# Rounding the feed-forward's gated tile in its own block instead of the next one

## The chip, the cores and the metric

The kernel runs on one core of a Trainium2 chip. The metric is device time in microseconds for one execution. All arithmetic is in 32-bit floats; matrix products are done as three products of split operands.

## What is computed

Two blocks of a network on 256 tokens of width 1024: a first block of two layers (a recurrent mixer in layer 0, a windowed attention in layer 1, each followed by a gated feed-forward part), and a second block with two kinds of attention on 16 further meta tokens. The change concerns the feed-forward part of both layers:

```python
D_MODEL = 1024
SEQ = 256
D_FF = -(-(8 * D_MODEL) // (3 * 256)) * 256      # 2816 = 11 blocks of 256

def swiglu(h, w_in, w_out):
    gu = h @ w_in
    gate, up = gu[..., :D_FF], gu[..., D_FF:]
    return (jax.nn.silu(gate) * up) @ w_out

x = x + swiglu(rmsnorm(x, norm_ffn_w[i]), ffn_w_in[i], ffn_w_out[i])
```

## The kernel before

The five engines have hand-written programs that meet in semaphores. Each engine works through its own list in order, so a wait also holds what stands behind it.

**Split operands.** Every operand of a product is a pair: a rounded part (hi) and what is left (the rest, lo). `mm3` (L472) issues three matmuls, hi by hi, hi by lo and lo by hi. ACT makes the hi part by a copy into the rounded type, DVE makes the lo part by a subtraction.

**Main weights** come in 56 chunks of 1024 x 512, each as two halves of 1 MB. SP loads a half into `w_raw` (one buffer for each half, `main`, L347) once DVE has made the rest of the same half of the chunk before; ACT rounds it into `w_hi` (`split_main`, L1210), DVE makes `w_lo` (`rest_main`, L1742). `w_hi` and `w_lo` have two slots. **Side units** are 128 x 1024 pieces, for the feed-forward's down projection two for each block; they have two slots too (`s_raw`, `s_hi`, `s_lo`), and SP loads the next one into a slot when DVE has made the rest of the one there (`side`, L352). SP's order is: both halves of a main chunk, then two side units, then the next chunk.

**The feed-forward part** has 11 blocks of 256 hidden features (`ffn` on each engine: L728 on TensorE, L1417 on ACT, L2089 on DVE). The order on TensorE (PE) is written out by hand: up(f+1), then down(f).

- `up(f)` (L740): 96 matmuls of 256 columns give gate and up rows of the block, for each of two halves of 128 features in one PSUM bank.
- ACT and DVE gate: DVE scales a half out of its bank into `ffn_nat` (L2097), ACT takes the silu in place (`gate`, L1423), DVE multiplies (L2103).
- The gated tile is `ffn_nat[:, 1]`. ACT rounds it into g_hi (`rounded`, L1430), DVE makes g_lo (`rested`, L2116). There is one such pair of tiles, so `rounded(f)` waits on `s_used` until down(f-1), which reads it, is over.
- `down(f)` (L751): waits for g_lo, then for each of the two side units waits for its s_lo and issues 12 matmuls of 512 columns into four banks that sum over all blocks. Each unit's last matmul signals `s_used`.

Block f on ACT and DVE (`block_`, L1432 and L2118) stands as: round and rest the gated tile of block **f-1**; gate block f; split the main chunk of block f+2; split the two side units of block f. The last block (f = 10) has a place of its own for its gated tile (`last_gh`, `last_gl`, in x_hi and x_lo) and its second side unit (`last_sh`, `last_sl`), and rounds the tile between the two side units:

```python
for s in range(2):
    slot = (u0 + s) % 2
    hi = s_hi[:, slot, :]
    if last and s:
        rounded(f, last_gh)
        hi = last_sh
    else:
        act.wait_ge(s_used, u0 + 2 * f + s - 2)
```

Behind the last block ACT and DVE split the next chunk (L1275, L1838), DVE adds the four banks into the residual h (L2152), and TensorE transposes h for what follows (L545), in the middle of `last_down` (L763).

Block 0 is written out before the loop, in the order gate, side units, round and rest, chunk 2.

Of the kernel before, what the change touches and what calls it, by code (L numbers as in the profile page):

```python
# [163 lines left out]
def two_blocks(nc, w_main, w_side, params, rows, c_l0, c_l1, c_b2, ident_d, x_d, x_t, meta_d, pos_d, out_d):  # L164
    ctx = ExitStack()
    with ctx:
# [40 lines left out]
        def side_raw(slot, quarters=False):  # L207
            return s_raw[:, slot, :].rearrange("p (k t) -> p k t", k=4) if quarters else s_raw[:, slot, :]
# [62 lines left out]
        last_gh, last_gl, last_sh, last_sl = x_hi[:, 2:4, M:L], x_lo[:, 2:4, M:L], x_hi[:, 4:8, M:L], x_lo[:, 4:8, M:L]  # L271
# [937 lines left out]
        def _(act):  # L1209
            def split_main(c, slot):  # L1210

                for g in range(2):
                    act.wait_ge(w_landed[g], 16 * c + 16)
                    act.activation(w_hi[:, slot, 4 * g:4 * g + 4, :], w_raw[:, g, :, :], ACT.Copy).then_inc(w_hi_ok, 1)  # L1214

            def split_side(u, after=None):

                act.wait_ge(s_landed[u % 2], 16 * (u // 2 + 1))
                if after is not None:
                    act.wait_ge(acc_ready[USE[after] % 2], USE[after] // 2 + 1)  # L1220
                act.activation(s_hi[:, u % 2, :], s_raw[:, u % 2, :], ACT.Copy).then_inc(s_hi_ok, 1)
# [51 lines left out]
            def split_half(c, slot, g):  # L1273
                act.wait_ge(w_landed[g], 16 * c + 16)
                act.activation(w_hi[:, slot, 4 * g:4 * g + 4, :], w_raw[:, g, :, :], ACT.Copy).then_inc(w_hi_ok, 1)  # L1275
# [134 lines left out]
            def meta_pairs():  # L1410

                for t, k0, k1 in ((meta_hi, 0, META_G), (meta_lo, META_G, KT)):
                    act.activation(t[:, :, 0:M], x_hi[:, k0:k1, 0:M], ACT.Copy)
                    act.activation(t[:, :, 2 * M:3 * M], x_lo[:, k0:k1, 0:M], ACT.Copy)
                act.drain().then_inc(xm_ok, 1)

            def ffn(layer, after):  # L1417
                c0, u0, n0 = C_FFN[layer], U_DOWN[layer], USE[(f"ffn{layer}", 0, 0)]

                def gate(f):  # L1420
                    for half in range(2):
                        act.wait_ge(acc_free[(n0 + half) % 2], (n0 + half) // 2 + f + 1)
                        act.activation(ffn_nat[:, 0, half, :], ffn_nat[:, 0, half, :], ACT.Silu).then_inc(silu_ok, 1)  # L1423

                def rounded(f, hi=ffh, first=False):

                    act.wait_ge(gated_ok, 2 * FB * layer + 2 * f + 2)
                    if not first:
                        act.wait_ge(s_used, u0 + 2 * f - 1)
                    act.activation(hi, ffn_nat[:, 1, :, :], ACT.Copy).then_inc(g_hi_ok, 1)  # L1430

                def block_(f, j, last=False, first=False):  # L1432
                    if not first:
                        rounded(f - 1)
                    gate(f)
                    if not last:
                        split_main(c0 + f + 2, (c0 + j) % 2)
                    for s in range(2):
                        slot = (u0 + s) % 2
                        hi = s_hi[:, slot, :]  # L1440
                        if last and s:
                            rounded(f, last_gh)
                            hi = last_sh
                        else:
                            act.wait_ge(s_used, u0 + 2 * f + s - 2)
                        act.wait_ge(s_landed[slot], 16 * (f + (u0 + s) // 2 + 1))
                        act.activation(hi, side_raw(slot, last and s), ACT.Copy).then_inc(s_hi_ok, 1)

                act.wait_ge(rb_ps, 1 + 2 * layer)
                act.activation(root_row, bank[6][:, 0:S], ACT.Copy).then_inc(root_ok, 1)  # L1450
                gate(0)
                for s in range(2):
                    split_side(u0 + s)
                rounded(0, first=True)
                split_main(c0 + 2, c0 % 2)
                block_(1, 1, first=True)
                if layer == 0:

                    act.wait_ge(meta_landed, 16)
                    act.activation(um[0:M, :], hm[0:M, :], ACT.Square, accum_out=stat[0:M, 0:1]).then_inc(ss_ok, 1)  # L1460
                else:
                    act.wait_ge(um_lo, 1)
                    meta_pairs()
                block_(2, 2)
                with act.Fori(1, (FB - 1) // 2 - 1) as i:
                    block_(2 * i + 1, 1)
                    block_(2 * i + 2, 2)
                if layer == 0:

                    act.wait_ge(ang_ok, 1)  # L1470
                    act.activation(sinT, ang[:, 0, :], ACT.Sin)
                    act.activation(cosT, ang[:, 1, :], ACT.Sin).then_inc(tab_ok, 1)

                block_(FB - 2, 1)
                block_(FB - 1, 2, last=True)
                for g in range(2):
                    split_half(c0 + FB + 1, c0 % 2, g)
                after()
# [13 lines left out]


            ffn(0, x1)

            acc_in(("ak",))
# [46 lines left out]
            def u_():  # L1543
# [18 lines left out]
                next_sides(1, (1,))  # L1562

            ffn(1, u_)


# [174 lines left out]
        def _(dve):  # L1741
# [162 lines left out]
            last = [P - 1, P]  # L1904
# [184 lines left out]
            def ffn(layer, first_tiles, after):  # L2089
# [24 lines left out]
                def rested(f, hi=ffh, lo=ffl):  # L2114
                    dve.wait_ge(g_hi_ok, FB * layer + f + 1)
                    dve.tensor_tensor(lo, ffn_nat[:, 1, :, :], hi, ALU.subtract).then_inc(g_lo_ok, 1)  # L2116

                def block_(f, j, last=False, first=False, between=None):  # L2118
                    if not first:
                        rested(f - 1)  # L2120
                    gated_halves(f, between)
                    if not last:
                        rest_main(c0 + f + 2, (c0 + j) % 2)
                    for s in range(2):
                        slot = (u0 + s) % 2
                        hi, lo = s_hi[:, slot, :], s_lo[:, slot, :]
                        if last and s:
                            rested(f, last_gh, last_gl)
                            hi, lo = last_sh, last_sl
                        dve.wait_ge(s_hi_ok, u0 + 2 * f + s + 1)  # L2130
                        dve.tensor_tensor(lo, side_raw(slot, last and s), hi, ALU.subtract).then_inc(s_lo_ok, 1)  # L2131
# [4 lines left out]
                    rest_side(u0 + s)  # L2136
                rested(0)
                rest_main(c0 + 2, c0 % 2)
                block_(1, 1, first=True)
                block_(2, 2, between=angles if layer == 0 else None)  # L2140
                with dve.Fori(1, (FB - 1) // 2 - 1) as i:
                    block_(2 * i + 1, 1)
# [573 lines left out]
```

## Time and profile before

| | |
|---|---|
| time, median of 3 runs | 954.61 us (954.53 to 956.06) |
| time of the profiled execution | 956.59 us |
| its span, from the first to the last instruction | 954.8 us |
| TensorE's matmuls (PE) busy | 97% of the span |
| DVE busy | 63% |
| ACT busy | 50% |
| bytes moved by DMA | 150.51 MB, 158 GB/s on average |

Times in the profile are microseconds from the start of the span. A timeline row has the start, the duration, the engine, the line of the kernel, the operation and, in brackets, how long the engine had been idle before it and what ended that. A matmul's own duration is modelled and overlaps the next one's; starts are the better reading. An idle engine costs nothing unless something that bounds the end waits for it. Layer 0's feed-forward stage runs from about 130 to 325 us, layer 1's from about 420 to 610.

### The profile page before, as it was taken

The numbers are of one execution on the slowest core, as the hardware profiler recorded it, in microseconds if no ns is written. First come the engines' busy times: TensorE is split into PE (matmuls) and PEld (weight loads), VectorE is DVE, ScalarE is ACT, GpSimd is POOL, SyncE is SP. The second block draws the span as 40 slices with busy tenths as digits, with TensorE's granted clock in tenths as the row PEclk, the third lists the DMA queues.
The fourth block names the chain that finished last, engine by engine and source line by source line (L and its number), as shares of the span: only waits on it lengthen the run. The fifth ranks groups of instructions, "written<-read, shape, count | busy, mean of one in ns | idle before, by whom it ended". The sixth has DMA issues, their size and how long they took to land.

```text
span 954.8 us, 15686 instructions
## 1 busy us (share of the span) xinstructions
PE 927.1 (97%) x6013; PEld 818.6 (86%) x6013; DVE 606.0 (63%) x1099; ACT 479.5 (50%) x781; POOL 38.8 (4%) x67
## 2 busy tenths in 40 slices
PE   6999899999999999999999999999999999999997
PEld 6887689999998798899999999789987878878776
DVE  5866857746557678557546556676665556565665
ACT  6555565334344547555334343677354454445443
POOL 1013200000000000000000000001011000000000
PEclk9999999999999999999999999999999999999999
DMA  8552346553644622236553644531523242533441
GB/s 310 207 184 81 108 176 220 181 217 132 233 162 155 243 89 90 89 131 220 180 217 132 223 173 164 189 132 71 199 90 134 89 162 104 176 119 126 176 176 44
DMA packets 26380, 150.51 MB, mean 158 GB/s; under 512 B 3664, under 2 KB 3920, under 8 KB 12112
## 3 DMA queue, kind: packets, MB, share of 16 engines
q1 hardware_dynamic: 24912, 147.44, 42.6%
q0 software_dynamic: 1408, 2.25, 0.8%
q8 instruction: 40, 0.66, 0.3%
q14 instruction: 20, 0.16, 0.1%
HBM read 148.50 MB, written 1.05 MB: 157 GB/s over the span
## 4 chain that ended last, share of the span: by engine, by line
PE 46%; DMA 18%; DVE 17%; ACT 10%; issue 4%; SPq 2%; DVEq 2%; ACTq 0%
DMA w_raw<-w_main_dram 18%; PE bank L474 12%; PE bank L476 11%; PE bank L475 11%; ACT w_hi L1214 5%; DVE s_lo L2131 4%; DVE w_lo L1746 4%; DVE w_lo L1838 2%; PE bank L545 1%; PE bank L1028 1%; DVE arena L2238 1%; SPq L345 1%; ACT w_hi L1275 1%; PE bank L1043 1%; PE bank L1081 1%
## 5 line engine op out<-in xcount | busy, mean ns | idle before, releaser
L474 PE MATMUL bank<-x_hi,w_hi 128*128 128x256 f32 (+1 forms) x976 | 279.2, 286 | 9.3 <-DVE w_lo L1848 8.0
L475 PE MATMUL bank<-x_lo,w_hi 128*128 128x256 f32 (+1 forms) x976 | 274.1, 281 | 0.0
L476 PE MATMUL bank<-x_hi,w_lo 128*128 128x256 f32 (+1 forms) x976 | 273.7, 280 | 0.0
L474 PEld LDWEIGHTS bank<-x_hi,w_hi 128*128 128x128 f32 x976 | 184.6, 189 | 13.0 <-issue 9.3
L1746 DVE TENSOR_TENSOR w_lo<-w_raw,w_hi 128x2048 fp32r<-128x2048 f32 x50 | 114.3, 2291 | 113.4 <-ACT w_hi L1214 112.8
L475 PEld LDWEIGHTS bank<-x_lo,w_hi 128*128 128x128 f32 x976 | 184.8, 189 | 0.8
L476 PEld LDWEIGHTS bank<-x_hi,w_lo 128*128 128x128 f32 x976 | 184.7, 189 | 0.0
L1214 ACT ACTIVATE w_hi<-w_raw 128x2048 fp32r<-128x2048 f32 x54 | 103.1, 1916 | 112.0 <-DMA w_raw<-w_main_dram 106.0
L474 PE MATMUL bank<-w_hi,x_hi 128*128 128x512 f32 (+2 forms) x296 | 119.1, 402 | 0.8 <-DVE w_lo L1746 0.8
L1838 DVE TENSOR_TENSOR w_lo<-w_raw,w_hi 128x2048 fp32r<-128x2048 f32 x51 | 116.2, 2283 | 5.5 <-ACT w_hi L1275 5.4
L475 PE MATMUL bank<-w_lo,x_hi 128*128 128x512 f32 (+2 forms) x296 | 112.6, 380 | 0.0
L476 PE MATMUL bank<-w_hi,x_lo 128*128 128x512 f32 (+2 forms) x296 | 112.5, 380 | 0.0
L1275 ACT ACTIVATE w_hi<-w_raw 128x2048 fp32r<-128x2048 f32 x50 | 95.1, 1907 | 17.2 <-DMA w_raw<-w_main_dram 16.7
L1423 ACT ACTIVATE ffn_nat<-ffn_nat 128x256 f32<-128x256 f32 x44 | 18.4, 418 | 108.3 <-DVE ffn_nat L2097 108.3
L474 PE MATMUL bank<-s_hi,g_hi 128*128 128x512 f32 x166 | 66.3, 399 | 2.4 <-DVE g_lo L2116 1.8
L474 PEld LDWEIGHTS bank<-w_hi,x_hi 128*128 128x128 f32 x296 | 55.8, 188 | 13.6 <-issue 4.1
L1504 ACT ACTIVATE arena<-arena,small 128x144 f32<-128x144 f32 x64 | 29.5, 461 | 74.4 <-DVE small L2215 74.3
L476 PE MATMUL bank<-s_hi,g_lo 128*128 128x512 f32 x166 | 65.5, 395 | 0.0
L476 PEld LDWEIGHTS bank<-w_hi,x_lo 128*128 128x128 f32 x296 | 55.6, 188 | 11.5
L475 PE MATMUL bank<-s_lo,g_hi 128*128 128x512 f32 x166 | 65.3, 393 | 0.0
L475 PEld LDWEIGHTS bank<-w_lo,x_hi 128*128 128x128 f32 x296 | 55.8, 189 | 8.6
L474 PE MATMUL bank<-w_hi,s_hi 128*128 128x512 f32 x128 | 53.2, 415 | 0.7 <-DVE h L2029 0.4
(378 smaller groups left out, 1436.5 us busy)
## 6 DMA issues: line engine op xcount, KB each, us to landing
w_raw<-w_main_dram SPq DMA_DIRECT2D x111, 1024.0 KB, 5.2
s_raw<-w_side_dram SPq DMA_DIRECT2D x51, 512.0 KB, 4.2
w_raw<-w_main_dram SPq DMA_DIRECT2D x2, 512.0 KB, 6.1
h<-x_dram SPq DMA_DIRECT2D x2, 512.0 KB, 10.5
arena<-rows_dram POOLq DMA_DIRECT2D x2, 512.0 KB, 4.3
arena<-x_t_dram SPq DMA_DIRECT2D x1, 768.0 KB, 6.7
out_dram<-arena SPq DMA_DIRECT2D x1, 512.0 KB, 2.6
out_dram<-arena SPq DMA_DIRECT2D x2, 256.0 KB, 2.1
```

The lines of the kernel that those rows point to most:

```text
L345: sp.dma_start(dst, w_main[c, g]).then_inc(w_landed[g], 16)
L474: pe.matmul(out, ah, bh, start=first, stop=False)
L475: pe.matmul(out, ah, bl, start=False, stop=False)
L476: return pe.matmul(out, al, bh, start=False, stop=last)
L545: ins = pe.transpose(b[:, M + r * P:M + (r + 1) * P], src(r, k), ident[:, :])
L1214: act.activation(w_hi[:, slot, 4 * g:4 * g + 4, :], w_raw[:, g, :, :], ACT.Copy).then_inc(w_hi_ok, 1)
L1275: act.activation(w_hi[:, slot, 4 * g:4 * g + 4, :], w_raw[:, g, :, :], ACT.Copy).then_inc(w_hi_ok, 1)
L1423: act.activation(ffn_nat[:, 0, half, :], ffn_nat[:, 0, half, :], ACT.Silu).then_inc(silu_ok, 1)
L1504: ins = act.activation(tiles(r), tiles(r), ACT.Exp, bias=small[:, s0 + 2 + r:s0 + 3 + r], accum_out=small[:, s0 + 4 + r:s0 + 5 + r])
L1746: dve.tensor_tensor(w_lo[:, slot, 4 * g:4 * g + 4, :], w_raw[:, g, :, :], w_hi[:, slot, 4 * g:4 * g + 4, :], ALU.subtract).then_inc(w_lo_o ...
L1838: dve.tensor_tensor(w_lo[:, slot, 4 * g:4 * g + 4, :], w_raw[:, g, :, :], w_hi[:, slot, 4 * g:4 * g + 4, :], ALU.subtract).then_inc(w_lo_o ...
L2131: dve.tensor_tensor(lo, side_raw(slot, last and s), hi, ALU.subtract).then_inc(s_lo_ok, 1)
```

## The change

The gated tile of block f is rounded and rested inside block f, right behind its gating, ahead of the main chunk and the side units, on ACT and on DVE. The last block does the same with its own tile, so there the rounding stands ahead of both side units. Block 0 stays as it was. What each instruction waits for is the same as before.

```diff
-                def block_(f, j, last=False, first=False):
-                    if not first:
-                        rounded(f - 1)
+                def block_(f, j, last=False):
                     gate(f)
-                    if not last:
+                    if last:
+                        rounded(f, last_gh)
+                    else:
+                        rounded(f)
                         split_main(c0 + f + 2, (c0 + j) % 2)
                     for s in range(2):
                         slot = (u0 + s) % 2
                         hi = s_hi[:, slot, :]
                         if last and s:
-                            rounded(f, last_gh)
                             hi = last_sh
                         else:
                             act.wait_ge(s_used, u0 + 2 * f + s - 2)
...
-                block_(1, 1, first=True)
+                block_(1, 1)
...
-                def block_(f, j, last=False, first=False, between=None):
-                    if not first:
-                        rested(f - 1)
+                def block_(f, j, last=False, between=None):
                     gated_halves(f, between)
-                    if not last:
+                    if last:
+                        rested(f, last_gh, last_gl)
+                    else:
+                        rested(f)
                         rest_main(c0 + f + 2, (c0 + j) % 2)
                     for s in range(2):
                         slot = (u0 + s) % 2
                         hi, lo = s_hi[:, slot, :], s_lo[:, slot, :]
                         if last and s:
-                            rested(f, last_gh, last_gl)
                             hi, lo = last_sh, last_sl
```

ACT's list at the first block of layer 0 and the head of its loop, before (w_hi: main chunk, s_hi: side unit, ffn_nat: silu, g_hi: rounding of the gated tile):

```order
 L1430 ACTIVATE g_hi<-ffn_nat 128x512
 L1214 ACTIVATE w_hi<-w_raw 128x2048 x2
 L1423 ACTIVATE ffn_nat<-ffn_nat 128x256 x2
 L1214 ACTIVATE w_hi<-w_raw 128x2048 x2
 L1447 ACTIVATE s_hi<-s_raw 128x1024 x2
```

and with the change:

```order
 L1430 ACTIVATE g_hi<-ffn_nat 128x512
 L1214 ACTIVATE w_hi<-w_raw 128x2048 x2
 L1423 ACTIVATE ffn_nat<-ffn_nat 128x256 x2
 L1430 ACTIVATE g_hi<-ffn_nat 128x512
 L1214 ACTIVATE w_hi<-w_raw 128x2048 x2
 L1447 ACTIVATE s_hi<-s_raw 128x1024 x2
```

The rounding of block 1 now stands between its silus and the split of the chunk; before, it followed the side units, as the first item of block 2.

ACT's list at the end of layer 0's feed-forward part, from the rounding of block 9 on, before (x_hi<-ffn_nat: rounding of the last gated tile, x_hi<-s_raw: the last side unit, w_hi at L1275: the next chunk):

```order
 L1430 ACTIVATE g_hi<-ffn_nat 128x512
 L1423 ACTIVATE ffn_nat<-ffn_nat 128x256 x2
 L1447 ACTIVATE s_hi<-s_raw 128x1024
 L1430 ACTIVATE x_hi<-ffn_nat 128x2x256
 L1447 ACTIVATE x_hi<-s_raw 128x4x256
 L1275 ACTIVATE w_hi<-w_raw 128x2048 x2
```

and with the change:

```order
 L1423 ACTIVATE ffn_nat<-ffn_nat 128x256 x2
 L1430 ACTIVATE x_hi<-ffn_nat 128x2x256
 L1447 ACTIVATE s_hi<-s_raw 128x1024
 L1447 ACTIVATE x_hi<-s_raw 128x4x256
 L1275 ACTIVATE w_hi<-w_raw 128x2048 x2
```

The rounding of block 9 has moved up into its own block, and the last rounding from between the two side units to ahead of both. DVE's rests (L2116, L1746, L2131) move in the same way in every block.

## Rows read from the trace of the kernel before

**Rows 1.** The page: busy time of the engines, and the chain that ended last.
```profile
PE 927.1 (97%) x6013; PEld 818.6 (86%) x6013; DVE 606.0 (63%) x1099; ACT 479.5 (50%) x781; POOL 38.8 (4%) x67
...
PE 46%; DMA 18%; DVE 17%; ACT 10%; issue 4%; SPq 2%; DVEq 2%; ACTq 0%
```

**Rows 2.** Timeline, TensorE: down(2)'s last matmul, down(3)'s first and last, layer 0.
```profile
195.20 0.39 PE L476 MATMUL bank<-s_hi,g_lo 128*128 128x512 f32 x1
...
206.66 0.39 PE L474 MATMUL bank<-s_hi,g_hi 128*128 128x512 f32 x1
...
211.98 0.39 PE L476 MATMUL bank<-s_hi,g_lo 128*128 128x512 f32 x1
```

**Rows 3.** Chain in order of time: start, duration, what; two flights are second halves.
```profile
215.19 1.93 ACT w_hi L1214
...
223.29 8.87 DMA w_raw<-w_main_dram
...
456.82 10.24 DMA w_raw<-w_main_dram
```

**Rows 4.** Timeline, ACT and DVE, the same block: first half, side rests, g_lo.
```profile
212.74 1.92 ACT L1214 ACTIVATE w_hi<-w_raw 128x2048 fp32r<-128x2048 f32 x1 [4.74 <-DMA w_raw<-w_main_dram]
...
219.35 2.35 DVE L2131 TENSOR_TENSOR s_lo<-s_raw,s_hi 128x1024 fp32r<-128x1024 f32 x2
221.62 0.68 DVE L2116 TENSOR_TENSOR g_lo<-ffn_nat,g_hi 128x512 fp32r<-128x512 f32 x1
```

**Rows 5.** TensorE's waits over the whole run: us in total, times, longest.
```profile
PE bank L474 <- DVE x_lo L2116: 3.0, 2, 1.5
PE bank L474 <- DVE g_lo L2116: 1.8, 4, 1.1
```

**Rows 6.** Timeline, TensorE: last matmul of down(0) and down(9), both layers.
```profile
161.64 0.39 PE L476 MATMUL bank<-s_hi,g_lo 128*128 128x512 f32 x1
...
314.57 0.40 PE L476 MATMUL bank<-s_hi,g_lo 128*128 128x512 f32 x1
...
446.70 0.39 PE L476 MATMUL bank<-s_hi,g_lo 128*128 128x512 f32 x1
...
599.87 0.40 PE L476 MATMUL bank<-s_hi,g_lo 128*128 128x512 f32 x1
```

**Rows 7.** Timeline, DVE: rest of the chunk's second half in block 1, both layers.
```profile
165.30 2.29 DVE L1746 TENSOR_TENSOR w_lo<-w_raw,w_hi 128x2048 fp32r<-128x2048 f32 x1 [0.73 <-ACT w_hi L1214]
...
450.65 2.29 DVE L1746 TENSOR_TENSOR w_lo<-w_raw,w_hi 128x2048 fp32r<-128x2048 f32 x1 [0.28 <-ACT w_hi L1214]
```

**Rows 8.** Timeline, ACT, DVE and TensorE: the last block of layer 0.
```profile
312.22 1.06 ACT L1447 ACTIVATE s_hi<-s_raw 128x1024 fp32r<-128x1024 f32 x1 [0.45 <-PE bank L476]
315.06 0.63 ACT L1430 ACTIVATE x_hi<-ffn_nat 128x512 fp32r<-128x512 f32 x1 [1.78 <-PE bank L476]
315.60 1.04 ACT L1447 ACTIVATE x_hi<-s_raw 128x1024 fp32r<-128x1024 f32 x1
316.54 1.90 ACT L1275 ACTIVATE w_hi<-w_raw 128x2048 fp32r<-128x2048 f32 x1
...
313.31 1.23 DVE L2131 TENSOR_TENSOR s_lo<-s_raw,s_hi 128x1024 fp32r<-128x1024 f32 x1 [1.08 <-ACT s_hi L1447]
...
320.69 1.28 DVE L2152 TENSOR_TENSOR h<-h,bank 128x512 f32<-128x512 f32 x2
...
316.47 0.50 PE L474 MATMUL bank<-s_hi,x_hi 128*128 128x512 f32 x1 [1.50 <-DVE x_lo L2116]
...
321.29 0.40 PE L476 MATMUL bank<-x_hi,x_lo 128*128 128x512 f32 x1
322.02 0.66 PE L545 MATMUL bank<-ident,h 128*128 128x128 f32 x4 [0.34 <-DVE h L2152]
```

**Rows 9.** Windows: length, busy us of the engines, PEclk, DMA share, GB/s.
```profile
8.00:14.00 6.00, 6.00 (x29) 6.00 (x30) 4.21 (x9) 3.98 (x9) 0.00 (x0) 1.00 1.02 418
...
314.00:318.00 4.00, 2.50 (x12) 1.54 (x10) 2.46 (x3) 2.94 (x3) 0.00 (x0) 1.00 0.99 408
```

More of the change, by code:

```diff
@@ L2138, in ffn @@
                 rest_main(c0 + 2, c0 % 2)
-                block_(1, 1, first=True)
+                block_(1, 1)
                 block_(2, 2, between=angles if layer == 0 else None)
```

## The prediction

> **What bounds the kernel now.** I read the page first, then the matmuls in order of time, then ACT, DVE and the waits of the feed-forward stages. TensorE is busy for 97% of the span, yet the chain that ended last gives 18% of the span to the loads of the main weights and 17% to DVE [rows 1]. Two things run at nearly one speed, then. Nothing outside the two feed-forward stages is touched, so the question is where TensorE stops inside them.
>
> *TensorE's pace.* The last matmul of one down projection starts at 195.20, that of the next at 211.98 [rows 2]: a block takes **16.78 us** when nothing is waited for.
>
> *The weight loop's pace.* A chunk's second half lands, ACT splits it (1.93 from 215.19 on), DVE takes the rest (from 1.95 after ACT's start), then the rests of both side units, and only behind these does SP issue the next loads: the next second half is on its way from 223.29 for 8.87 and lands at 232.16, when ACT can start again, 0.03 later [rows 3]. That is a round of **17.00 us**. The loop falls behind TensorE by 0.22 us a block, and by more where a flight takes longer (10.24 in layer 1 [rows 3]).
>
> *What ends the waits.* The rest of the gated tile, g_lo, is DVE's last item in that loop: it ends at 222.30, and TensorE wants it at 223.44 [rows 4]. As the loop falls behind, this margin goes. TensorE waits for g_lo four times, up to 1.1 us [rows 5]. The whole loss is read better from first and last matmul: layer 0 from 161.64 to 314.57 is 152.93 us for nine blocks, where nine times 16.78 is 151.02, so 1.91 us lost; layer 1 from 446.70 to 599.87 is 153.17, so 2.15 us [rows 6]. Behind that each layer has one wait of 1.5 us for x_lo, the last gated tile [rows 5].
>
> **The change part by part.** No arithmetic is added or taken away: in each layer the roundings and rests of blocks 1 to 9 (18 of each in all) and of the last block (2 of each) move. PE, SP and POOL keep their order. A rounding takes ACT 0.63 us [rows 8], a rest takes DVE 0.68 [rows 4].
>
> *The gain: g_lo comes before the wait that mattered.* Let the lead be ACT's start on a second half minus the start of the last matmul of the down projection before it: 215.19 - 211.98 = 3.21. TensorE reaches the next down projection 11.46 after that matmul (195.20 to 206.66 [rows 2]). Before, it needs g_lo, which ends 222.30 - 215.19 = 7.11 after ACT's start and is seen 0.05 later, so it stalls once the lead passes 11.46 - 7.16 = 4.30. Afterwards g_lo is long there, and what ends last is the rest of the **first side unit**. It ends 219.35 + 1.23 - 215.19 = 5.39 after ACT's start [rows 4, 8], so the stall begins at a lead of 11.46 - 5.44 = 6.02. (The second unit is wanted 12 matmuls, some 2.8 us, later and is 1.2 us behind the first: never last.) That is 1.72 us more room in each layer.
>
> *The price inside the loop: the first block.* `rounded(f)` waits for the down projection of f-1 to be over, since it overwrites the tile that this reads. ACT sees that end 0.49 us after the last matmul's start (314.57 to 315.06 [rows 8]). Behind it ACT now holds the split of the next chunk. With the rounding on ACT for 0.54 before the next start (315.06 to 315.60), that split cannot start earlier than 1.03 after the last matmul. In steady blocks this costs nothing: 211.98 + 1.03 = 213.01 against 212.74, and the second half is not ready before 215.19 anyway [rows 4]. DVE then takes the second half's rest at the old time, to 0.01 us. But in block 1 the loads came early, as the loop had just started. In layer 0 the first half was split as soon as it had landed, now at 161.64 + 1.03 = 162.67; DVE starts that rest 1.95 later, at 164.62, and the second at 166.83 (a rest takes 2.29, and the next item starts 0.08 before its end, as 221.62 against 221.70 [rows 4]), where it was 165.30: **1.53 us**. In layer 1: 446.70 + 1.03 = 447.73, rests at 449.68 and 451.89 instead of 450.65: **1.24 us** [rows 6, 7]. The loop feeds itself (the side rests are late, so SP issues late), so the delay stays in it for the other eight blocks.
>
> So the stalls are 1.91 + 1.53 - 1.72 = 1.72 us in layer 0 and 2.15 + 1.24 - 1.72 = 1.67 in layer 1. **Gains: 0.19 and 0.48.** Bounds: nothing if the flights grow a little, 1.72 per layer if the loop catches up after block 1. I take the middle of the mechanism, since [rows 3] show no slack in the loop.
>
> *The price in the last block.* Before, ACT splits the block's first side unit (s_hi) during the down projection, at 312.22, and the rounding into x_hi follows at 315.06. TensorE restarts at 316.47, 1.90 after its last matmul (314.57), on x_lo. Now the rounding stands first and still waits for the down projection's end. Counted from 314.57: rounding 0.49 to 1.12, s_hi 1.03 to 2.09; on DVE x_lo 1.15 to 1.84 and s_lo 2.12 to 3.35 [rows 8]. TensorE restarts at 3.40 instead of 1.90: **1.50 us later**, waiting for s_lo. Some of it is covered: at 322.02 (7.45) TensorE waited for DVE's sum into h, though its own work would have let it go on at 321.29 + 0.23, 6.95 (0.23 is the step of the 512-column matmuls, 5.32 us for 23 of them [rows 2]). Now its own work brings it there at 8.45. The sum is queued behind the split of the next chunk, which ACT starts 0.94 later (one more unit ahead of it) and DVE too, so it ends at 7.40 + 0.94 = 8.34. TensorE goes on at 8.45 instead of 7.45: **1.0 us late**. I take 1.0 per layer, with bounds 0.9 and 1.5 and nothing to take off, since behind it TensorE is full [rows 1].
>
> *SP's queue.* The next layer's side loads are issued behind those rests, and come some 2 us later; the main load behind them waits for the chunk's rest and moves by 0.94 with it. That is inside the 1.0 already.
>
> *Sum:* -0.19 - 0.48 + 1.0 + 1.0 = **+1.3 us**. The profiled execution took 956.59 us around a span of 954.8; by the sum it would be 957.9 and the span 956.1. The runs' median is 954.61, 2 us under the profiled one, so the forecast is **955.9 us**. That is 0.14% and would not be told from no change: 0.2%, about 1.9 us, is what a measurement of this kernel can tell.
>
> **A rule of the skill against the row.** The gaps of TensorE end on g_lo, and the edit makes just that value earlier [rows 5]. The Trainium skill, Perfetto Trace Analysis, section Optimization Strategy, says to look at the gaps of the limiting engine, find the signal that ends them and let what sends it start sooner; read so, the stalls of 4.06 us would be the gain. The trace disagrees in part: the loop of [rows 3], not g_lo, falls behind.
>
> **The rivals.**
> - *B, the loop catches up.* The delay of block 1 is not carried, because flights after it are shorter. Against it: the loop's round of 17.00 has no idle step in it. For it: in layer 1 the flight after block 1 took 10.24 [rows 3], so something disturbs it that a shift might miss. Then 1.72 is recovered twice: -3.44 + 2.0 = -1.4 us, 953.2. With the last block covered as well, -3.4 us, 951.2.
> - *S, the last block is paid in full (slower).* Place: the restart on s_lo behind block 10. If the sum into h ends half a microsecond later than worked out, the cover is gone and 1.50 counts twice: 3.0 - 0.7 = +2.3 us, 956.9; with no stall recovered +3.0, 957.6. It decides from 1.3 us a layer on. For it: the sum stands only 0.1 us ahead of TensorE, behind five queued items on DVE. Against it: their times repeat to 0.01 us in both layers.
> - *C, the clock.* TensorE's gap there grows from 1.9 to 3.4 us from start to start. The granted clock reads 1.00 (the 2.4 GHz level) in the stretch with the present gap. It does in the first stretch too, though there 29 matmuls take 6.00 us, 0.21 each [rows 9], where 96 of them take 11.46 - 0.23, 0.12 each [rows 2]. If the longer gap brought that slow stretch back, 29 x (0.21 - 0.12) = 2.6 us more per layer: 1.3 + 5.2 = +6.5 us, 961.1. The Trainium skill, TensorE: Matmul & The Clock Gate, section Why this matters for your kernels, warns that idle gaps between bursts return the engine to its slow level. No row here shows it in a running stage.
> - *N, nothing changes in effect,* because TensorE still meets the second limit each time: 954.6.
>
> **How the numbers follow.** Forecast 0.52, S 0.22, B 0.13 and its far form 0.05, C 0.04, N 0.04. Of the forecast's own spread 0.04 lies over 0.2% slower; of B 0.02 over 0.2% faster. So slower 0.22 + 0.04 + 0.04 = 0.30, faster 0.05 + 0.02 = 0.07, the same 0.63. The range holds B to S with the run-to-run spread: 952.9 to 957.8.
>
> **What would show it.** In the new trace: ACT's split of the first half in block 1 starts about 1.0 us behind the last matmul of the down projection, and the lead in block 2 is 1.2 to 1.5 us larger than it was; leads reach 6 and more by block 8; TensorE's waits before down projections name s_lo, not g_lo, and still sum to about 1.7 us a layer; the last down projection starts 3.4 us after the one before ended, on s_lo; h comes 1 us later. I am wrong if the leads fall back after block 2 (B), if TensorE goes on 1.5 us late after the last block (S), or if matmuls behind it start further apart than 0.23 us (C).

## The result, and the profile after

| | before | after |
|---|---|---|
| median of the runs, us | 955.02 (951.15 to 956.06, 6 runs) | 960.18 (958.46 to 963.0, 6 runs) |
| ratio to before | | 1.006 (95%: 1.0037 to 1.0083) |
| profiled execution: time, span, us | 956.59, 954.8 | 958.46, 956.7 |
| mean granted clock, mean of the runs | 0.9991 | 0.9943 |
| stages (last matmul of down(0) to that of down(9)), us | 152.93, 153.17 | 151.02, 151.48 |
| TensorE's restart behind down(9), us after its start | 1.90, 1.90 | 3.47, 3.48 |
| first transpose of h, counted likewise, us | 7.45, 7.45 | 9.98, 9.29 |

The change makes the kernel slower by 0.6%, 5.2 us; 955.9 with a range up to 957.8 was forecast. The profiled execution of the changed kernel is the fastest of its six, so the traces show only 1.9 us of it. Clock means here and below are over all executions of a kernel in its comparison; the one for before is over the 30 that ran beside experiments 1 to 4.

The page: TensorE as busy as before, but the chain that ended last now runs over TensorE for 63% and over the loads for 11%, where it was 46% and 18% [rows 1]. In the middle of the stages nothing but TensorE sets the pace.
```profile
PE 927.2 (97%) x6013; PEld 819.7 (86%) x6013; DVE 605.7 (63%) x1099; ACT 480.3 (50%) x781; POOL 38.8 (4%) x67
...
PE 63%; DVE 12%; DMA 11%; ACT 7%; issue 3%; DVEq 2%; SPq 1%; ACTq 0%
```

Timeline, TensorE: the last matmuls of down(0) and down(9) in both layers, as in [rows 6].
```profile
162.45 0.39 PE L476 MATMUL bank<-s_hi,g_lo 128*128 128x512 f32 x1
...
313.47 0.39 PE L476 MATMUL bank<-s_hi,g_lo 128*128 128x512 f32 x1
...
448.07 0.39 PE L476 MATMUL bank<-s_hi,g_lo 128*128 128x512 f32 x1
...
599.55 0.40 PE L476 MATMUL bank<-s_hi,g_lo 128*128 128x512 f32 x1
```
Layer 0 takes 151.02 us, which is nine times 16.78 with no stall at all; layer 1 takes 151.48. Against [rows 6] the stages gain 1.91 and 1.69 us. And yet from down(9) of layer 0 to down(0) of layer 1 it is 134.60 us instead of 132.13, so 2.47 lost, and from down(9) of layer 1 to the end of the span 357.15 instead of 354.93, 2.22 lost. A further 0.81 is lost ahead of down(0), in a stretch that the edit doesn't touch (over the twelve traces of this case down(0) ends anywhere from 160.31 to 162.51). -1.91 + 2.47 - 1.69 + 2.22 + 0.81 = +1.9, the difference of the spans. So, apart from that 0.81, all that is lost is lost behind the two last blocks.

TensorE's waits: us in total, times, longest. The rows of x_lo and of L2116's g_lo [rows 5] are gone, and one for s_lo has come.
```profile
PE bank L474 <- DVE s_lo L2131: 6.2, 2, 3.1
...
PE bank L545 <- DVE h L2152: 0.7, 1, 0.7
```

Timeline, ACT and DVE, block 1 of layer 0, then ACT's split of the second half in block 9.
```profile
162.94 0.63 ACT L1430 ACTIVATE g_hi<-ffn_nat 128x512 fp32r<-128x512 f32 x1 [2.30 <-PE bank L476]
163.47 3.71 ACT L1214 ACTIVATE w_hi<-w_raw 128x2048 fp32r<-128x2048 f32 x2
163.60 0.69 DVE L2116 TENSOR_TENSOR g_lo<-ffn_nat,g_hi 128x512 fp32r<-128x512 f32 x1 [2.51 <-ACT g_hi L1430]
165.41 4.49 DVE L1746 TENSOR_TENSOR w_lo<-w_raw,w_hi 128x2048 fp32r<-128x2048 f32 x2 [1.11 <-ACT w_hi L1214]
...
300.82 1.92 ACT L1214 ACTIVATE w_hi<-w_raw 128x2048 fp32r<-128x2048 f32 x1 [0.54 <-DMA w_raw<-w_main_dram]
```
The rounding holds the split until 163.47, which is 1.02 after the matmul of 162.45 (1.03 was worked out). The two rests start 2.96 and, 2.2 later, some 5.17 behind it; the second was at 3.66 [rows 6, 7], so the push is 1.51 us, as forecast (1.53). It isn't carried in this trace, though. The lead (ACT's second split behind the last matmul of the down projection before) is 3.14 in block 2 and 300.82 - 296.69 = 4.13 in block 9, where before it rose from 2.01 to 5.57. In layer 1 it goes from 3.73 to 6.01 in block 8 and 6.18 in block 9, and behind these two stand the stalls that are left, 0.16 and 0.30 us. So TensorE stalls from a lead of about 5.87 on, where 6.02 was worked out; in the kernel before a lead of 5.57 went with a stall of 1.38, a limit of 4.19 where 4.30 was worked out. The room between the two limits is 1.68, as forecast (1.72).

Timeline, the last block of layer 0, ACT and DVE, then TensorE. Its counterpart is [rows 8].
```profile
313.95 0.63 ACT L1430 ACTIVATE x_hi<-ffn_nat 128x512 fp32r<-128x512 f32 x1 [4.05 <-PE bank L476]
314.49 1.04 ACT L1447 ACTIVATE s_hi<-s_raw 128x1024 fp32r<-128x1024 f32 x1
314.62 0.69 DVE L2116 TENSOR_TENSOR x_lo<-ffn_nat,x_hi 128x512 fp32r<-128x512 f32 x1 [4.26 <-ACT x_hi L1430]
315.44 1.04 ACT L1447 ACTIVATE x_hi<-s_raw 128x1024 fp32r<-128x1024 f32 x1
315.56 1.23 DVE L2131 TENSOR_TENSOR s_lo<-s_raw,s_hi 128x1024 fp32r<-128x1024 f32 x1 [0.26 <-ACT s_hi L1447]
...
316.94 0.47 PE L474 MATMUL bank<-s_hi,x_hi 128*128 128x512 f32 x1 [3.08 <-DVE s_lo L2131]
317.71 0.39 PE L474 MATMUL bank<-s_hi,x_hi 128*128 128x512 f32 x1
317.94 0.59 PE L475 MATMUL bank<-s_lo,x_hi 128*128 128x512 f32 x1
318.32 0.63 PE L476 MATMUL bank<-s_hi,x_lo 128*128 128x512 f32 x1
318.75 0.63 PE L474 MATMUL bank<-x_hi 128*128 128x512 f32 x1
...
321.31 0.43 PE L474 MATMUL bank<-s_hi,x_hi 128*128 128x512 f32 x1
321.58 0.40 PE L475 MATMUL bank<-s_lo,x_hi 128*128 128x512 f32 x1
```
Item by item this is what was worked out: the rounding waits for the down projection, s_hi and s_lo queue up behind it, and TensorE restarts 316.94 - 313.47 = 3.47 later (3.40). What was not in the sum comes next. The first matmuls follow each other at 0.23, and from 317.94 on at 0.43, eight of them, until 321.31; then at 0.23 again. That stretch costs 321.31 - 317.94 - 8 x 0.23 = 1.5 us. Below, matmuls that start that far apart are called slow.

Windows of the changed kernel: length, busy us of the engines, granted clock (the third number from the end), DMA share, GB/s.
```profile
314.00:318.00 4.00, 1.06 (x5) 0.92 (x6) 3.05 (x3) 4.00 (x4) 0.00 (x0) 1.00 0.57 215
318.00:322.00 4.00, 4.00 (x12) 3.13 (x11) 2.74 (x2) 2.08 (x2) 0.00 (x0) 0.58 0.84 268
```
The granted clock in the window behind the gap is 0.58: mostly the lower of its two levels (0.50, 1.2 GHz), for the rest the full one (1.00, 2.4 GHz). In the same four microseconds TensorE is called fully busy, which is why its busy share on the page tells nothing.

Timeline, the same place in layer 1, where the clock stayed up.
```profile
603.35 1.92 ACT L1275 ACTIVATE w_hi<-w_raw 128x2048 fp32r<-128x2048 f32 x1 [0.78 <-DMA w_raw<-w_main_dram]
605.30 2.29 DVE L1838 TENSOR_TENSOR w_lo<-w_raw,w_hi 128x2048 fp32r<-128x2048 f32 x1 [1.28 <-ACT w_hi L1275]
607.51 1.28 DVE L2152 TENSOR_TENSOR h<-h,bank 128x512 f32<-128x512 f32 x2
608.84 0.33 PE L545 MATMUL bank<-ident,h 128*128 128x128 f32 x1 [0.73 <-DVE h L2152]
```
Here ACT waits 0.78 for the next main chunk to land, DVE's rest of it is late by that, and the sum into h is queued behind that rest. h is transposed at 9.29 instead of the 8.45 worked out.

So three things were to be told apart: the longer path of the last block, the clock, and the landing of the next chunk.

### The profile page after: what moved, and what is told of

It is laid out like the page before. It is cut to its first block, busy times and chain, and to the rows that moved or that the text cites. A ratio compares the mean times of both kernels' runs of the same rounds, so it can differ in the third digit from the quotient of the medians.

```text
span 956.7 us, 15686 instructions
## 1 busy us (share of the span) xinstructions
PE 927.2 (97%) x6013; PEld 819.7 (86%) x6013; DVE 605.7 (63%) x1099; ACT 480.3 (50%) x781; POOL 38.8 (4%) x67
## 4 chain that ended last, share of the span: by engine, by line
PE 63%; DVE 12%; DMA 11%; ACT 7%; issue 3%; DVEq 2%; SPq 1%; ACTq 0%
PE bank L474 18%; PE bank L475 17%; PE bank L476 17%; DMA w_raw<-w_main_dram 11%; ACT w_hi L1214 3%; DVE w_lo L1838 2%; DVE s_lo L2131 2%; DVE w_lo L1746 2%; PE bank L545 1%; PE bank L1028 1%; DVE arena L2238 1%; PE bank L1043 1%; PE bank L1081 1%; PE bank L885 1%; PE bank L1063 1%
## 5 line engine op out<-in xcount | busy, mean ns | idle before, releaser
L1746 DVE TENSOR_TENSOR w_lo<-w_raw,w_hi 128x2048 fp32r<-128x2048 f32 x50 | 114.0, 2291 | 49.9 <-ACT w_hi L1214 49.4
L1275 ACT ACTIVATE w_hi<-w_raw 128x2048 fp32r<-128x2048 f32 x50 | 95.0, 1907 | 19.1 <-DMA w_raw<-w_main_dram 18.6
```

Of the source, the lines that this page charges most:

```text
L1746: dve.tensor_tensor(w_lo[:, slot, 4 * g:4 * g + 4, :], w_raw[:, g, :, :], w_hi[:, slot, 4 * g:4 * g + 4, :], ALU.subtract).then_inc(w_lo_o ...
```

## The experiments

Four kernels ran beside 30 executions of the kernel before (955.25 median, 952.46 to 958.44), then four beside 27 (956.01, 952.27 to 959.61), then two beside 17 (955.36, 953.12 to 959.44). What a version costs against before is counted from the median beside which it ran. All diffs are against the kernel before unless said otherwise. In some kernels line numbers differ by up to five. "Restart" is TensorE's first matmul of the last down projection and "h" the first transpose of h, both counted from the last matmul of down(9) as in the table above.

**1. Only the inner half of the edit (blocks 1 to 9).** The last block keeps its old order.
```diff
-                def block_(f, j, last=False, first=False):
-                    if not first:
-                        rounded(f - 1)
+                def block_(f, j, last=False):
                     gate(f)
                     if not last:
+                        rounded(f)
                         split_main(c0 + f + 2, (c0 + j) % 2)
```
with `rested` moved in the same way on DVE.

> Blocks 1 to 9 as changed, the last block in its old order. Theory (path and clock): the inner blocks save the stalls (1.9 us in layer 0, 1.7 in layer 1 in the profiled execution of the change), the last block keeps its gap of 1.9 us, and no clock is lost: about 955.0 - 3.6 = 951.4 us, granted clock as before. Rival (the inner order itself is slower in most executions, through longer flights of the weights): 957 us or more.

Measured: 956.67 us, ratio 1.0022 (1.0007 to 1.0037). My theory missed: this half alone makes the kernel slower by 1.4 us. The stages do take 151.50 and 151.67, so 1.43 and 1.50 us of stall are gone, and TensorE restarts at 1.90 as before. But h is transposed at 9.08 and 8.57 instead of 7.45, which gives back 1.63 and 1.12 of the 2.93 (one trace of each kernel). Timeline of this kernel, behind the last block of layer 0 (its last matmul of the down projection starts at 312.33), and a window behind that:
```profile
315.92 1.92 ACT L1275 ACTIVATE w_hi<-w_raw 128x2048 fp32r<-128x2048 f32 x1 [1.52 <-DMA w_raw<-w_main_dram]
317.87 2.29 DVE L1837 TENSOR_TENSOR w_lo<-w_raw,w_hi 128x2048 fp32r<-128x2048 f32 x1 [2.21 <-ACT w_hi L1275]
...
321.41 0.66 PE L545 MATMUL bank<-ident,h 128*128 128x128 f32 x4 [1.97 <-DVE h L2150]
```
```profile
322.00:327.00 5.00, 4.75 (x25) 4.29 (x24) 2.55 (x5) 1.65 (x4) 0.00 (x0) 0.66 0.43 180
```
TensorE arrives earlier, the load doesn't. The wait that was in front of the down projections stands behind the last block instead. And after the two gaps there (1.51 on x_lo, 1.97 on h) the granted clock fell too, to 0.66 over five microseconds, which cost 1.5 us more in this execution. Over its 12 executions the mean clock is 0.9978 against 0.9991; by an estimate that takes the lost clock as lost time, (0.9991 - 0.9978) x 955 = 1.2 us, about what the kernel is slower by.

The same trace shows a lead unlike that of the changed kernel, with the same inner order. ACT's split of the second half in blocks 2 and 9 of layer 0:
```profile
181.43 1.92 ACT L1214 ACTIVATE w_hi<-w_raw 128x2048 fp32r<-128x2048 f32 x1 [0.49 <-DMA w_raw<-w_main_dram]
...
301.41 1.92 ACT L1214 ACTIVATE w_hi<-w_raw 128x2048 fp32r<-128x2048 f32 x1 [0.54 <-DMA w_raw<-w_main_dram]
```
The down projections before them end at 177.61 and 295.26, so the lead goes from 3.82 to 6.15, where the changed kernel had 3.14 and 4.13.

**2. Only the last block's half of the edit.** On ACT, and likewise with `rested` on DVE:
```diff
-                    if not last:
+                    if last:
+                        rounded(f, last_gh)
+                    else:
                         split_main(c0 + f + 2, (c0 + j) % 2)
...
                         if last and s:
-                            rounded(f, last_gh)
                             hi = last_sh
```

> Only the last block as changed, blocks 1 to 9 in the old order. Theory (path and clock): TensorE's gap before the last down projection is 3.4 us in both layers, 1.6 us longer each, and the granted clock falls behind it in some executions; if the parts add up, 5.2 + 3.6 = 8.8 us over the kernel before, about 963.8 us, of which some 3.3 is the path and the rest clock. Path without clock: 958.3 us. Rival (the inner order is what costs): 955 to 956.5 us.

Measured: 960.28 us, ratio 1.0047 (1.0029 to 1.0064), the greater part of the whole change's 1.006. Alone this half costs 5.0 us; the sum of parts that I expected (963.8) is 3.5 too high, and the path without clock (958.3) is 2.0 too low. Restart at 3.47 in both layers, h at 9.76 and 11.23. Two lines of TensorE in layer 0, then a window in layer 1:
```profile
318.51 0.76 PE L474 MATMUL bank<-s_hi,x_hi 128*128 128x512 f32 x1 [3.08 <-DVE s_lo L2133]
319.07 0.63 PE L475 MATMUL bank<-s_lo,x_hi 128*128 128x512 f32 x1
```
```profile
606.00:608.00 2.00, 2.00 (x6) 1.58 (x5) 1.61 (x2) 2.00 (x2) 0.00 (x0) 0.50 0.85 266
```
In layer 1 the granted clock reads 0.50 in whole stretches, the lower level exactly. The slow matmuls cost 1.4 us in layer 0 and 2.8 in layer 1.

**3. The change, with the last rounding not waiting.** The wait protects the tile that the down projection before still reads. In the last block the rounding writes into another one (`last_gh`, a part of x_hi), so it needs no such wait. Against the changed kernel:
```diff
                     if last:
-                        rounded(f, last_gh)
+                        rounded(f, last_gh, first=True)
```

> The change, but the last block's rounding no longer waits for the down projection before it (its tile of its own does not need that wait), so it runs right behind the gating. Theory: TensorE's gap before the last down projection goes from 3.4 us to under 0.5, part of it moves to the wait for the sum into h; 1.2 us a layer less than with the old last block: about 949 us, granted clock as before. Rival (the inner order costs): 955 us or more.

Measured: 957.61 us, ratio 1.0023 (1.0009 to 1.0037), 8.6 above the expectation and in the rival's range. The gap did close, with restarts at 0.43 and 1.63. But TensorE then waits for the sum into h, 1.76 us in layer 0 and 3.27 in layer 1, and the sum is queued behind the late load. Timeline, layer 1:
```profile
607.08 0.65 PE L545 MATMUL bank<-ident,h 128*128 128x128 f32 x4 [3.27 <-DVE h L2152]
```
A gap of 3.27 on h has taken the place of the one that was removed, and slow matmuls follow it (608.04 to 611.47, 1.3 us).

**4. The change, with the gap filled.** Against the changed kernel, 12 matmuls of 512 columns ahead of the last down projection, into a bank that is free there. Their result isn't used.
```diff
                 def last_down(f):
+                    spare = w_hi[:, (c0 + FB) % 2, 0, :]
+                    pe.wait_ge(w_lo_ok, 2 * (c0 + FB) + 1)
+                    for _ in range(12):
+                        pe.matmul(bank[2][:, :], spare[:, 0:P], spare, start=True, stop=True)
                     pe.wait_ge(g_lo_ok, FB * layer + f + 1)
```

> The change, with 12 matmuls of 512 columns into an idle bank ahead of the wait of the last down projection (their result is not used), 2.8 us of work in a gap of 3.4 us. Clock theory: the path is as in the change, but the engine does not stand idle: about 954.7 to 956 us, granted clock 0.998 or more in every execution. Rival (the clock is no part of it, the 5.2 us are path): 960 us, as the change.

Measured: 956.44 us, ratio 1.0013 (1.0001 to 1.0026), where the change alone has 1.006. That is 1.2 us over before where the change has 5.2: 4.0 us are won by work of no use, which changes no wait and no order on ACT and DVE (3.7 between the two medians as they stand). The granted clock is 0.998 or more in all executions but the profiled one, which is the slowest of the 12 (0.997). Timeline and window behind the filled gap in layer 0; the last down projection itself restarts at 3.47, as in the change:
```profile
315.65 0.47 PE L474 MATMUL bank<-s_hi,x_hi 128*128 128x512 f32 x1 [0.34 <-DVE s_lo L2135]
```
```profile
318.00:322.00 4.00, 3.94 (x19) 2.76 (x18) 2.96 (x5) 1.67 (x3) 0.00 (x0) 1.00 0.76 227
```
h is transposed at 8.40, against 8.45 worked out. In layer 1 a late load still opens gaps further on (h at 10.59), and 1.4 us of slow matmuls follow there.

**5. Where the delay comes from: the order of the loads.** No edit of ACT or DVE. SP issues the next main chunk ahead of the two side units, and not behind them.
```diff
+                main(c0)
                 with sp.Fori(0, FB - 1) as i:
-                    main(c0 + i)
+                    main(c0 + i + 1)
                     for s in range(2):
                         side(u0 + 2 * i + s, (u0 + s) % 2)
```
(behind the loops, the main chunk that they have already issued is left out).

> The kernel before, with SP issuing the next main chunk ahead of the two side units in the feed-forward loops (nothing else). Theory W (the round main load, split, rests, side rests, next load is what falls behind TensorE, and it only hands its delay from place to place): the next chunk is issued about 4.7 us earlier in each round, so the stalls before the down projections go in the old order too, 1.9 + 2.1 us, and the last block keeps its gap of 1.9 us: about 951 us. Rival G (the late g_lo itself is the cause, as the change assumes): 955 us, stalls as before.

Measured: 952.43 us (951.83 to 953.23), ratio 0.9967 (0.9954 to 0.9981), faster than the kernel before, 1.4 above theory W and 2.6 below rival G. Both stages take 151.02 us, with g_lo still in its old place. TensorE's waits, then ACT and SP in the timeline:
```profile
PE bank L475 <- DVE x_lo L2117: 3.0, 2, 1.5
```
```profile
207.56 3.71 ACT L1215 ACTIVATE w_hi<-w_raw 128x2048 fp32r<-128x2048 f32 x2
...
224.34 3.71 ACT L1215 ACTIVATE w_hi<-w_raw 128x2048 fp32r<-128x2048 f32 x2
```
```profile
211.96 2.53 SPq L345 DMA_DIRECT2D w_raw<-w_main_dram  x2
215.30 1.47 SPq L354 DMA_DIRECT2D s_raw<-w_side_dram  x2
```
In the kernel before, the same block:
```profile
220.75 1.47 SPq L354 DMA_DIRECT2D s_raw<-w_side_dram  x2
222.77 0.85 SPq L345 DMA_DIRECT2D w_raw<-w_main_dram  x2
```
There SP stood at the side units until DVE had made their rests (219.35 and on [rows 4]) and came to the main chunk only then. Now ACT waits for no load; it waited 4.74 for the first half before [rows 4]. The round is 224.34 - 207.56 = 16.78, TensorE's own, where the loop had 17.00 [rows 3]. A kernel whose weight loop has room shows no stall on g_lo.

**6. The change on that load order.** Diffs of the change and of 5 together.

> The change with the same new order on SP. Theory W: no stall in the blocks, gap of 3.4 us before the last down projection, h 8.4 us behind it, clock lost as in the change: 951 + 2 (path of the last block) + 4 (clock) = about 957 us, and in the profile leads that no longer grow over the blocks. Rival G: 960 us, as the change.

Measured: 957.24 us, ratio 1.001 (0.9997 to 1.0023), so the change costs 4.8 us on this kernel also. Stages 151.02, restarts 3.47, h at 9.97 and 11.09, slow matmuls behind both gaps (1.5 and 2.7 us), as theory W had it. With no stall left to recover, only the last block's loss remains, and it is nearly as large as the change's 5.2 on the old order.

**7. That, with the last rounding not waiting.** Diffs of 6 and 3 together.

> As the run before, and the last block's rounding without the wait for the down projection. Theory W: no stall in the blocks, restart within 0.5 us, h about 7 us behind the end of the down projection: 951 - 2 x 0.5 = about 950 us if the clock holds, 952 if it falls in some executions. Rival G: 957 us, as the change with that wait gone.

Measured: 948.88 us (947.37 to 949.57), ratio 0.9921 (0.9902 to 0.9941). Restarts at 0.29 and 0.58, h at 5.43 and 5.70, no slow matmuls behind; 1.1 us under the 950 that was expected.

**8. Only the last block's half, with its gap filled.** Diffs of 2 and 4 together; the fillers' result isn't used.

> Only the last block as changed (blocks 1 to 9 old), with 12 matmuls of 512 columns filling TensorE's gap. Clock theory: the 3.4 us gap is bridged, the path cost of about 1 us a layer stays: 957 us, granted clock as in the kernel before. If the cost of the last block is all path: 960 us, as without the filling.

Measured: 957.0 us, ratio 1.0011 (0.9996 to 1.0025), where 2 had 1.0047, as the clock theory had it. The last down projection itself restarts at 3.48 in both layers, h at 8.42 and 8.45. The window in layer 1 that read 0.50 in 2:
```profile
606.00:608.00 2.00, 2.00 (x10) 1.65 (x9) 2.00 (x2) 1.78 (x1) 0.00 (x0) 1.00 0.89 272
```
TensorE is busy all of the two microseconds in both; it starts 10 instructions here and 6 there.

**9. The new load order with the inner half of the edit.** Diffs of 5 and 1 together.

> The kernel before with SP issuing the main chunk ahead of the side units, and the half of the change that lies in blocks 1 to 9 (the last block in the old order). Theory (the weight loop is what let TensorE fall behind, and with the loads in the new order the loop keeps up whatever the place of g_lo): both stages 151.0 us, no wait for g_lo, restart 1.90 behind the last down projection, time as the same load order without the edit, 952.4, within 1 us. Rival (the early g_lo is worth something by itself): 951 or less. Other rival (the split held behind the end of the down projection costs also here): 954 or more.

Measured: 952.41 us (951.56 to 953.5), ratio 0.9973 (0.9961 to 0.9985); stages 151.01 and 151.02, h at 7.45. The same as 5 within the intervals: an early g_lo is worth nothing once the loop keeps up, and costs nothing.

**10. The new load order, old inner order, last block rounded early without the wait.** Version 7 less its inner half.

> The new load order, the old order in blocks 1 to 9, and the last block as changed but with its rounding not waiting for the down projection before it. Theory (all that the best version gains over the load order comes from the last block): 948.9 within 1 us, stages 151.0, restart 0.3 to 0.6, no slow matmuls behind it. Rival (the inner half carries part of it): 950.5 or more.

Measured: 947.51 us (946.77 to 948.38), ratio 0.9923 (0.9903 to 0.9944), 1.4 under the expected 948.9, so a little outside its 1 us; it can't be told from 7. The page's chain, and TensorE at the end of layer 0's stage:
```profile
PE 82%; DVE 8%; ACT 5%; DMA 2%; DVEq 2%; issue 1%; ACTq 0%; SPq 0%
```
```profile
311.81 0.39 PE L477 MATMUL bank<-s_hi,g_lo 128*128 128x512 f32 x1
312.04 0.39 PE L475 MATMUL bank<-s_hi,x_hi 128*128 128x512 f32 x1
```
The last down projection follows the one before it at 0.23, with no gap, and h comes at 5.09 in both layers, 2.36 us earlier than in the kernel before. Twice that is 4.7, and from 9 to 10, which ran in one comparison, it is 4.9.

The three kernels with the open gap of 3.47 us (the change, 2 and 6), each with the one that differs from it in the filling or the wait alone, then 1 and the kernel before. In 4 and 8 the last down projection still restarts at 3.47 to 3.48, and the fillers start at 0.23. The kernel before had a mean clock of 0.9987 and 0.9988 in the later two comparisons.

| kernel | next matmul behind down(9), us | ratio to before | mean clock of its runs |
|---|---|---|---|
| the change | 3.47, 3.48 | 1.006 | 0.9943 |
| 4, the change, gap filled | 0.23, 0.23 | 1.0013 | 0.9988 |
| 2, last block alone | 3.47, 3.47 | 1.0047 | 0.9953 |
| 8, the same, filled | 0.23, 0.23 | 1.0011 | 0.9991 |
| 6, the change on the new load order | 3.47, 3.47 | 1.001 | 0.9955 |
| 7, the same, no wait | 0.29, 0.58 | 0.9921 | 0.9988 |
| 1, inner half alone | 1.90 | 1.0022 | 0.9978 |
| before | 1.90 | 1 | 0.9991 |

## Why the prediction was wrong

*The gain.* The mechanism held: with g_lo early, TensorE stalls later (limits 5.87 and 4.19, for 6.02 and 4.30). The term was mis-sized. The step that failed is "The loop feeds itself (the side rests are late, so SP issues late), so the delay stays in it for the other eight blocks": block 1 was pushed by 1.51 us, as worked out, yet by block 9 the lead of layer 0 was 4.13 and not 5.57 + 1.5. The stalls shrank by 3.6 us together, not by 0.67. In this trace it went as rival B said. How far the push is carried differs between executions: in experiment 1's trace the lead did grow to 6.15. With the early g_lo the stalls of both layers are 0.46 us (the change), 1.13 (1), 1.44 (3) and 2.04 (4), with the old order 4.06 (before), 3.61 (2) and 3.59 (8), one trace each; the sum had 3.39, more than any of the four. What B left out, and my sum too, is that the loop hands on what it is late by: the chunk behind the last block lands no sooner. Experiment 1 has it alone: 2.9 us of stall gone, 2.75 back behind the last block in the same trace, and 1.4 us slower by the medians. The sentence in the prediction that the loop "of [rows 3], not g_lo, falls behind" was right, and experiments 5 and 9 show it: moving the loads removes every stall, moving g_lo on top of that is worth nothing that can be measured (952.43 and 952.41). I should have drawn the conclusion that a stall taken away ahead of a late loop is not a gain at all until something behind the loop is free of it.

*The last block.* The path was right to 0.07 us: restart 3.47 (3.40), h at 8.40 to 8.45 where clock and load didn't interfere (8.45), on s_lo in place of x_lo. Experiment 8, which has this term and no fallen clock, costs 1.0 us (-0.4 to 2.4) where 2.0 was forecast for it, which the interval holds; 4, the change with the clock held up behind the restart, costs 1.2, against +1.3 for the whole sum. That last agreement is partly luck, since its terms are others than mine. Rival S, a path paid in full, didn't happen: the cover held.

*The clock.* This is the step that failed and made the result fall out of the range. "The granted clock reads 1.00 (the 2.4 GHz level) in the stretch with the present gap" was taken as a reason against rival C, with 0.04. It says nothing of a gap of 3.4 us. C's mechanism is what the windows show: the lower level, from the restart on or within 1.2 us of it. Filling the gap with work of no use wins 4.0 us in the change (5.2 against 1.2) and 4.0 in its last block alone (5.0 against 1.0; by the ratios, 1.0047 against 1.0011, it is 3.4; in neither pair do the intervals overlap), and it brings the mean clock from 0.9943 and 0.9953 back to 0.9988 and 0.9991. The clocks give the same size: with matmuls 0.43 apart instead of 0.23, about half of the slow time is lost, so by an estimate (0.9988 - 0.9943) x 960 = 4.3 us and (0.9991 - 0.9953) x 960 = 3.6 us. C's price was 2.6 us per layer, worked out from the slow first stretch; the traces show 1.4 to 2.8 us, and behind five of the six open gaps of 3.47 us in the traces of the change, 2 and 6 (the changed kernel's layer 1 has none). C's 961.1 is 0.9 from the median of 960.18. The rule of the Trainium skill, TensorE: Matmul & The Clock Gate, section Why this matters for your kernels, that idle gaps between bursts bring the engine back to its slow level, agrees with the 0.58 behind the 3.08 us of waiting; I had cited it and then weighed it by a row that couldn't test it.

*The sum as it is.* Of 5.2 us by the medians, the clock is 4.0 (the change against 4) and the rest 1.2. The profiled execution, the fastest, shows only 1.9 of the 5.2: its stages gained 3.6, the stretches behind them lost 4.7, of which 1.5 is slow matmuls, and 0.8 was lost ahead of them.

*Still open.* Why the push of block 1 was not carried in layer 0 of the changed kernel and was in experiment 1. In which execution a gap of 3.5 us lets the clock fall, and in which layer; I have one trace of each kernel and only the mean clock of the others. Why waits for h do it too in some places and not in others: slow matmuls follow waits of 1.97 (1, layer 0), 2.01 (4, layer 1) and 3.27 (3, layer 1), and none follow 1.43 (1, layer 1) and 1.76 (3, layer 0). No experiment varied these alone, and filling them wasn't tried. That the clock's fall explains all of the 4.0 us in the change rests on the fill acting through nothing else; restart and h in 4 and 8 are as worked out wherever the load isn't late, which speaks for it.

## What to carry to other kernels

If a signal that ends the limiting engine's gaps is the last item of a slower loop, moving the item only moves the wait; compare the loop's round with the engine's (17.00 against 16.78 here) and look for what lengthens the round. Here SP had two small loads ahead of a large one, and stood waiting to issue the small ones while the large one could have gone. A TensorE gap has a price beyond its length: growing one from 1.9 to 3.5 us was to cost 1.0 us per layer on the path, and cost some 1.7 to 2.0 more in clock (experiments 2 and 8, 3.4 to 4.0 us for two layers). When an item is moved ahead of others, take along only the waits that its data need: the last block's move with a needless wait left out, on the better load order, is in the two fastest versions here (947.5 and 948.9 us, ratios 0.9923 and 0.9921). Leaving out that wait was worth 8.4 us there (7 against 6), and 2.8 on the old load order (3 against the change), where the late load took the rest.

## What the runs showed of the hardware

- The granted clock read 1.00 around a wait of 1.5 us [rows 9], and 0.50 to 0.60 in windows behind one of 3.08 us (0.58 in the change, 0.50 in 2). Matmuls of 512 columns then start 0.43 apart instead of 0.23, for 3 to 6 us, after which the full level is back though TensorE has worked without a stop.
- It fell behind shorter waits too: 0.66 over 322 to 327 us behind 1.97 us in experiment 1, and 0.73 over 608 to 613 behind 2.01 us in 4.
- Behind the restart the engine still ran at full pace for 1.0 us in the changed kernel (316.94 to 317.94) and for 1.2 in 6, layer 0; in experiment 2 it was at the low one from the restart on (318.51).
- The column isn't a full account either: in 8 to 14 us it reads 1.00 [rows 9] while matmuls of 256 columns start 0.21 apart, the same spacing as behind experiment 1's gaps (323.75 to 323.96), where the window reads 0.66. The spacing of like matmuls is the surer sign.
- The page's busy share doesn't show it: 927.2 us (97%) with the slow stretch, 927.1 (97%) without [rows 1]. The mean granted clock of an execution does, in its third digit.
- With the old load order the executions of the kernel before spread over up to 7.3 us (952.27 to 959.61, 27 of them), with the new one over 1.4 (5, 10 executions) and 1.9 (9, 12 executions).
